# Sixteen transfers of v per pair instead of 28, four of them begun by ScalarE; scores in 32-query tiles; transposing writes turned into strided reads

## What is computed

```python
def hybrid_layer(x, g, w_in, rpb, w_dw, b_dw, ln_g, ln_b, w_pw, b_pw, w_out, pos):
    h = rms_norm(x, g)
    z = h @ w_in                                   # 1024 -> 3712 columns
    aq, ak, av, ag, bq, bk, bv, bg, ca, cb, cg = jnp.split(z, splits, axis=-1)
    ya = neighbourhood_attention(heads(aq, 4), heads(ak, 4), heads(av, 4), rpb) * silu(ag)
    yb = dilated_attention(rotary(heads(bq, 6), pos), rotary(heads(bk, 6), pos), heads(bv, 6)) * silu(bg)
    yc = conformer_conv(ca, cb, w_dw, b_dw, ln_g, ln_b, w_pw, b_pw) * silu(cg)
    return x + jnp.concatenate([ya, yb, yc], axis=-1) @ w_out
```

## Time and profile before

| | us |
|---|---|
| median of 3 runs | 555.41 |
| lowest, highest | 553.13, 556.37 |
| profiled execution, its own time | 554.33 |
| its span, first to last instruction | 552.7 |

### The profile page before, as it was taken

The page is one execution under the profiler, slowest core; times in us unless marked ns, Lnnn a source line. Parts: engine busy times, 40 slices in busy tenths (PEclk is TensorE's granted clock), DMA queues, the critical chain, the costliest instruction groups (busy, mean ns, idle before and its releaser), DMA issues.

```text
span 552.7 us, 9207 instructions
## 1 busy us (share of the span) xinstructions
PE 511.9 (93%) x3422; PEld 412.4 (75%) x3422; DVE 366.2 (66%) x733; ACT 244.9 (44%) x483; POOL 163.7 (30%) x224
## 2 busy tenths in 40 slices
PE   8999989399699999999999999948969999999995
PEld 7888767377587777778888877736748778787884
DVE  6889788389686486611639877773995866653333
ACT  6622355146255565523513215631643644763223
POOL 0113333112023555524411323221211335664201
PEclk9999999699899999999999999987999999999999
DMA  8626779637769698999503568882575979989973
GB/s 292 264 76 166 176 180 222 131 92 166 178 160 239 149 266 178 241 219 285 154 0 110 121 145 188 212 175 73 131 180 151 219 165 263 266 193 240 215 184 152
DMA packets 61931, 99.69 MB, mean 180 GB/s; under 512 B 25152, under 2 KB 38976, under 8 KB 61888
## 3 DMA queue, kind: packets, MB, share of 16 engines
q0 software_dynamic: 19648, 62.93, 50.7%
q1 hardware_dynamic: 41952, 36.00, 22.5%
q10 hardware_dynamic: 288, 0.19, 0.2%
HBM read 84.92 MB, written 4.72 MB: 162 GB/s over the span
## 4 chain that ended last, share of the span: by engine, by line
PE 76%; DMA 8%; issue 7%; DVE 5%; POOL 1%; SPq 1%; ACT 1%; POOLq 0%; DVEq 0%; ACTq 0%
PE acc L626 17%; PE acc L627 16%; PE acc L628 16%; DMA sq<-sq 4%; PE sc L742 3%; DMA w_lo<-w_out 3%; PE tp L765 3%; PE misc L796 2%; PE misc L791 2%; PE sc L688 1%; SPq L506 1%; PE sc L690 1%; PE sc L689 1%; PE sc L626 1%; PE sc L628 1%
## 5 line engine op out<-in xcount | busy, mean ns | idle before, releaser
L626 PE MATMUL acc<-act_hi,w_hi 128*128 128x512 f32 x480 | 194.3, 405 | 0.9 <-DMA w_lo<-w_out 0.9
L627 PE MATMUL acc<-act_hi,w_lo 128*128 128x512 f32 x480 | 187.6, 391 | 0.0
L628 PE MATMUL acc<-act_lo,w_hi 128*128 128x512 f32 x480 | 187.1, 390 | 0.0
L626 PEld LDWEIGHTS acc<-act_hi,w_hi 128*128 128x128 f32 x480 | 90.2, 188 | 22.1 <-issue 3.5
L628 PEld LDWEIGHTS acc<-act_lo,w_hi 128*128 128x128 f32 x480 | 90.2, 188 | 19.7
L627 PEld LDWEIGHTS acc<-act_hi,w_lo 128*128 128x128 f32 x480 | 90.3, 188 | 17.0 <-issue 0.5
L891 ACT ACTIVATE w_lo<-w_hi 128x1024 fp32r<-128x1024 f32 (+1 forms) x62 | 62.0, 1000 | 66.1 <-DMA w_hi<-w_out 39.2
L1316 DVE SCALAR_TENSOR_TENSOR y<-ub,par,y 128x512 f32<-128x512 f32 x90 | 68.1, 757 | 0.0
L953 ACT ACTIVATE prob<-prob,nmx 128x384 f32<-128x384 f32 (+1 forms) x80 | 45.2, 566 | 43.4 <-DVE nmx L1338 43.4
L1094 POOL DMA_DIRECT2D w_lo<-w_in x40 | 36.2, 905 | 94.9 <-ACT w_lo L891 94.3
L1316 DVE SCALAR_TENSOR_TENSOR ub<-ub,par 128x512 f32<-128x512 f32 x84 | 62.7, 747 | 0.0
(11 more groups left out here) (149 smaller groups left out, 756.0 us busy)
## 6 DMA issues: line engine op xcount, KB each, us to landing
w_hi<-w_in POOLq DMA_DIRECT2D x40, 512.0 KB, 5.3
w_lo<-w_in POOLq DMA_DIRECT2D x40, 512.0 KB, 6.1
w_hi<-w_out POOLq DMA_DIRECT2D x16, 512.0 KB, 6.7
w_lo<-w_out POOLq DMA_DIRECT2D x16, 512.0 KB, 7.0
pT<-w_in SPq DMA_DIRECT2D x15, 512.0 KB, 4.0
sq<-sq SPq DMA_DIRECT2D x48, 64.0 KB, 2.6
gf<-nabias SPq DMA_DIRECT2D x20, 128.0 KB, 5.4
v_way<-vs SPq DMA_DIRECT2D x8, 256.0 KB, 6.0
```

What stands on the lines that cost most here:

```text
L626: nc.tensor.matmul(to[:, :], w_hi[:, slot, k, :], a_hi[:, k, :], start=i == 0, stop=False)
L627: nc.tensor.matmul(to[:, :], w_lo[:, slot, k, :], a_hi[:, k, :], start=False, stop=False)
L628: last = nc.tensor.matmul(to[:, :], w_hi[:, slot, k, :], a_lo[:, k, :], start=False, stop=i == K - 1)
```

## The change

It has five parts.

- **Layout of v in HBM and the store.** `v_way` now keeps, for each of 32 rows, the four blocks of 32 partitions side by side. The store is four transfers of 32 partitions in place of one of 128.
- **Near loads.** SyncE's queue issues 12 transfers of a dilated pair, as before in shape, and no far ones.
- **Far loads.** `load_far` puts four transfers (32 partitions by 16 pieces of 32 elements each) in ScalarE's queue, at n = 6, 14 and 18 behind `norm`, in place of 16 on SyncE's. They go to a buffer of their own, `v_far`, and `values` waits for `far_moved` as well.
- **Scores.** Every product of scores is made for 32 queries at a time; near and far of one block follow each other.
- **Strided reads.** Seven access patterns on VectorE (v and the neighbourhood keys when emptied, rotated q and k) are walked in the order of the destination, so that they write neighbours and read with a step.

```diff
-        v = sb("v", [P, 2, 4, (NA_BLOCKS + CLASSES) * BLK])
+        v = sb("v", [P, 2, 4, NA_BLOCKS * BLK])
+        v_far = sb("v_far", [P, 2, 4, CLASSES * BLK])
-        v_way = nc.dram_tensor("v_way", (DEPTH, PAIRS, P, SEQ), F32, kind="Internal").ap()
+        v_way = nc.dram_tensor("v_way", (DEPTH, PAIRS, BLK, P // BLK, SEQ), F32, kind="Internal").ap()
...
         def by_class(t):
-            return t.rearrange("p (r a) -> p a r", r=CLASSES)
+            return t.rearrange("p (r a) -> p r a", r=CLASSES)
         def in_order(t):
-            return t.rearrange("p (a r) -> p a r", r=CLASSES)
+            return t.rearrange("p (a r) -> p r a", r=CLASSES)
...
             def store_v(l, g):
                 sp.wait_ge(v_blocks, PAIRS * l + g + 1)
-                sp.dma_start(v_way[l, g], v_buf(g)).then_inc(v_stored, 16)
+                for i in range(QUADS):
+                    sp.dma_start(v_way[l, g, :, i, :], v_buf(g)[BLK * i:BLK * (i + 1), :]).then_inc(v_stored, 16)
...
-                        t = v_way[l, g].rearrange("(i p) (r j c) -> j i p r c", p=BLK, r=CLASSES, j=QUADS)[j]
-                        for i in range(QUADS):
-                            sp.dma_start(to[:, i, FAR].rearrange("p (r c) -> p r c", r=CLASSES), t[i])\
-                                .then_inc(v_moved[g % 2], 16)
...
+                def product(b, r, h, first, end, keys_of):
+                    own, rows = slice(HD * h, HD * (h + 1)), slice(BLK * r, BLK * (r + 1))
+                    return nc.tensor.matmul(sc[2 * (b % 2) + h][rows, first:end],
+                                            queries[own, g % 2, b * P + BLK * r:b * P + BLK * (r + 1)],
+                                            keys_of(keys[own, g % 2, :]), start=True, stop=True)
...
+                        for r in range(CLASSES):
+                            for h in range(2):
+                                product(b, r, h, 0, NEAR, near)
+                        for r in range(CLASSES):
+                            for h in range(2):
+                                last = product(b, r, h, NEAR, DKEY, lambda t: t[:, P * r:P * (r + 1)])
                                 if r == CLASSES - 1:
+                                    last.then_inc(s_ready, 1)
...
                 if g < DPAIRS:
+                    pe.wait_ge(far_moved[g % 2], 16 * QUADS * (DPAIRS - 1 - g % 2) * l + 16 * QUADS * (g // 2 + 1))
...
+            def load_far(l, g):
+                act.wait_ge(v_stored, V_STORED * (PAIRS * l + g + 1))
+                if g >= 2:
+                    act.wait_ge(pv_done, PAIRS * l + g - 1)
+                elif l:
+                    act.wait_ge(pv_done, PAIRS * (l - 1) + DPAIRS)
+                for j in range(QUADS):
+                    t = v_way[l, g].rearrange("p i (r j c) -> j p (i r) c", r=CLASSES, j=QUADS)[j]
+                    act.dma_start(v_far[BLK * j:BLK * (j + 1), g % 2].rearrange("p i (r c) -> p (i r) c", r=CLASSES), t)\
+                        .then_inc(far_moved[g % 2], 16)
...
                     if 0 < n <= UNITS:
                         norm(l, n - 1)
+                    if n - 1 in V_LOADS and V_LOADS[n - 1] < DPAIRS:
+                        load_far(l, V_LOADS[n - 1])
```

More of the change, by code:

```diff
@@ L269, in build @@
         v_moved = [sem(f"v_moved{i}") for i in range(2)]
+        far_moved = [sem(f"far_moved{i}") for i in range(2)]
         x_blocks = sem("x_blocks")
@@ L390, in build @@
         NEAR_EVEN, NEAR_ODD = slice(0, QT * BLK), slice(QT * BLK, NA_BLOCKS * BLK)
-        FAR = slice(NA_BLOCKS * BLK, (NA_BLOCKS + CLASSES) * BLK)
+        V_STORED = 16 * QUADS
         def v_moves(g):
-            return (3 + QUADS) * QUADS if g < DPAIRS else QUADS
+            return 3 * QUADS if g < DPAIRS else QUADS
         def v_landed(l, g):
@@ L509, in store_v @@
                 sp.wait_ge(v_blocks, PAIRS * l + g + 1)
-                sp.dma_start(v_way[l, g], v_buf(g)).then_inc(v_stored, 16)
+                for i in range(QUADS):
+                    sp.dma_start(v_way[l, g, :, i, :], v_buf(g)[BLK * i:BLK * (i + 1), :]).then_inc(v_stored, 16)
             def load_v(l, g):
-                sp.wait_ge(v_stored, 16 * (PAIRS * l + g + 1))
+                sp.wait_ge(v_stored, V_STORED * (PAIRS * l + g + 1))
                 if PAIRS * l + g >= 2:
@@ L520, in load_v @@
                         low = NEAR_ODD.stop - NEAR_ODD.start
[L521 removed]
+                        t = v_way[l, g].rearrange("p i (j c) -> j p i c", j=QUADS)
                         sp.dma_start(to[:, :, NEAR_EVEN], t[j]).then_inc(v_moved[g % 2], 16)
@@ L731, in scores, with near @@
                     pe.wait_ge(m_ready, UNITS * l + n)
+                def product(b, r, h, first, end, keys_of):
[3 more added lines that the diff above has]
+                                            keys_of(keys[own, g % 2, :]), start=True, stop=True)
                 for b in range(b, b + 2):
[L734 to L737, removed]
+                    if g < DPAIRS:
+                        def near(t):
@@ L738, in scores @@
                             t = t.rearrange("p (r a) -> p r a", r=CLASSES)[:, :, NEAR_LO[b]:NEAR_LO[b] + 2 * PCLS]
[L739 to L747, removed]
+                            return t.rearrange("p r (u a) -> p u r a", u=2)
                         for r in range(CLASSES):
                             for h in range(2):
[L750 to L753, removed]
+                                product(b, r, h, 0, NEAR, near)
@@ L754, in scores @@
+                        for r in range(CLASSES):
+                            for h in range(2):
+                                last = product(b, r, h, NEAR, DKEY, lambda t: t[:, P * r:P * (r + 1)])
                                 if r == CLASSES - 1:
+                                    last.then_inc(s_ready, 1)
+                    else:
+                        for r in range(QUADS):
+                            for h in range(2):
+                                last = product(b, r, h, 0, NKEY,
+                                               lambda t: t[:, ROWS * NA_LO[b]:ROWS * NA_LO[b] + NKEY])
+                                if r == QUADS - 1:
@@ L790, in values @@
                         for i in range(QUADS):
-                            nc.tensor.matmul(of_class(ob[BLK * i:BLK * (i + 1), :], r), v_of(g, i, far_block(r)),
+                            nc.tensor.matmul(of_class(ob[BLK * i:BLK * (i + 1), :], r), v_far[:, g % 2, i, BLK * r:BLK * (r + 1)],
                                              of_class(pT[:, BLK * i // HD, 2, :], r), start=r == 0, stop=False)
@@ L1257, in empty_tile @@
                     if before is not None and before[0] >= 0:
-                        dve.wait_ge(v_stored, 16 * (PAIRS * before[0] + before[1] + 1))
+                        dve.wait_ge(v_stored, V_STORED * (PAIRS * before[0] + before[1] + 1))
                     nc.vector.transpose(v_blocked(g), vT.rearrange("p (m j t) -> p m j t", m=v_blocked(g).shape[1],
@@ L1347, in turn_p @@
                 if u == 0 and q == 2:
-                    dve.wait_ge(v_stored, 16 * PAIRS * (l + 1))
+                    dve.wait_ge(v_stored, V_STORED * PAIRS * (l + 1))
                 to = p_turned(q).rearrange("p (j u h t) -> p u h j t", j=QUADS, u=BATCH, t=BLK)[:, u]
```

12 lines of the change are left out of this document (5 added, 7 removed).

## The result

The changed kernel takes 530.3 us (median of 4, 525.61 to 532.15) beside 555.89 us of the kernel before on the same chip: ratio 0.952, 95% interval 0.943 to 0.961. The forecast was 524 us, range 515 to 539, and a faster kernel. The profiled execution took 528.64 us, its span is 526.8. One execution further down, 547.77 us of the kernel with all transfers on SyncE, was in a slower state of the chip and is left out of every number here.

A forecast was written before the change was run, and what follows sets the result against it. Bound: TensorE waiting for 28 transfers issued one behind the other. 554.3 - 28.9 (waits) - 6.9 (clock) + 1.5 (remaining wait) + 4.4 (ScalarE) - 1.7 (scores) = 522.7 us; as median 524 us, range 515 to 539.

The forecast's parts named there:

- The rival without effect: Before `values`: the wait is for the bank or the transposed probabilities, not v, so 555 us; chance 0.03.
- The clock: Matmuls of `values` behind the four waits: 17.98 us falls to 4 x 2.76 at full clock, -6.9 us.
- The near loads: SyncE's 12 near loads keep their shape: 1.6 us a group, 6.3 us for four, issued by 91.3 from 84.96.
- The remaining wait: Before the products of `values`: 1.5 us left for the whole program, bounds 0 and about 3 us per wait.
- What ScalarE pays: Store wait and four issues of 0.6 us delay the emptying of transposes: 2.2 us per layer, +4.4 us in all.
- I take 84.5: At n = 6: assumed time when the store of pair 0 has landed, making ScalarE 0.5 us late for the transposes.
- The slower rival: ScalarE's queue: issues of X us lose 12 X - 7 a layer; X = 2.3 gives 559 us; chance 0.03.
- The scores: Dilated pairs' score calls: one group of one form saves 0.14 us in each of 12 calls, -1.7 us.
- The strided reads: VectorE's strided SBUF reads: possibly 11 us of work saved, but TensorE never waits for it, so counted 0.
- The rival built on it: VectorE: each strided SBUF operand costs 0.4 us, an instruction 1.5 instead of 1.1; 530 us; chance 0.05.
- VectorE's cover: Without pair 1's wait VectorE is some 2 us behind but catches up by the scores: 0, bounds 0 and +6 us.
- One more sign: Sign of being right: SyncE's loads end some 12 us earlier relative to the first product of `values`.

The follow-up runs named there:

- the kernel with the later products: Changed kernel with far transfers one slot later and `values` of pairs 0 and 1 in the middle of the next half tile, gating behind taps: 522.10 us, ratio 0.940.

## Why the prediction was right, and where its terms were off

**What bounded the kernel** was named rightly. The wait before the products was the issuing of 28 transfers on one queue: with 16 on the same queue it is 17.0 us, with 12 there 2.1. The kernel with all 28 transfers on two queues, the last of them issued at 95.7 instead of 103.7 us, has no such wait, though TensorE also comes there later. The rival without effect is out.

**The clock** (-6.9 us) came as forecast where the waits went, 2.76 us at 1.00. What the step left out is that it works for any long wait: the new 4.18 us at the transposes cost 1.4 us behind them, and the kernel with 16 issues on ScalarE is some 12 us longer than its waits alone would make it.

**The near loads** were set at 0.58, 0.43 and 0.43 us; eleven of the twelve take 0.59 to 0.61 and one 0.67, so 7.7 us with the gaps instead of 6.3. It is the new layout in HBM, and not the second queue, that makes the small ones longer: their medians are 0.59 to 0.60 with all on SyncE as well, and 0.48 and 0.49 in the kernel with the old layout and two queues. The remaining wait was put at 1.5 us and is 2.1.

**What ScalarE pays** is the term that was mis-sized: +4.4 us forecast, +8.9 measured (10.5 less 1.6). The prediction names transposes that wait "for over 10 us in total" as a sign of being wrong; that sign came in the profiled execution, and was just missed (9.8) in the second one. An issue of 512 pieces was rightly taken at 0.6 us (median 0.649), and the number of pieces hardly counts. The wrong step was "I take 84.5" for the landing of the store of pair 0: it landed at 87.05. So TensorE waits 4.18 us behind n = 6 of the first layer where 0.5 was forecast. In that place the late landing is 2.5 of the 3.7 us between; 0.3 are the issues (2.88 instead of 2.6), and 0.8 come from TensorE, which got there at 87.38 instead of 88.15. This execution had the longest landing: 9.8 us from the first issue of the store to the first load, where the nine other profiled executions with a four-part store have 7.5 to 8.6. The forecast had 7.1. At the other places the waits are 1.25 (forecast 1.7) and 0.64 (0), and 1.09, 1.44 and 0.67 in the second layer, where 2.2 for all three was forecast. The 0.64 and 0.67 at n = 18 are the same term: the four-part store of pair 2 landed at 138.2 and held ScalarE there too. The 1.25 at n = 14 came without the wait for the store that the forecast had in it (landing at 127): the store had landed before ScalarE was free, and the issues and what stands behind them make it up.

**The slower rival** was priced by the right sum. Its 12 X - 7 us for a layer, with 16 issues of 0.65 us in place of four of X = 2.6, gives 24 x 2.6 - 14 = 48 us; the kernel made so waits 44.6 us in these places and is 3% slower than before. It didn't come to pass in the changed kernel because an issue of 512 pieces costs 0.65 us and not 2.2, and there are four of them.

**The scores** (-1.7 us) are right: 1.51 us a call where 1.52 was forecast, -2.0 us alone.

**The strided reads** (0) are right in the time. The mechanism had been left open, but "L1222 near 0.7 us" was named as a sign of being right, and it did not come: a read from SBUF with a step of 16 bytes costs nearly as much as the scattered write that it replaces. L1237 takes 1069 ns, L1222 took 1098:

```profile
L1237 DVE SCALAR_TENSOR_TENSOR vs<-acc,rstd 128x512 f32<-128x512 f32 x6 | 6.4, 1069 | 0.0
```

The rule of the Trainium skill ("SBUF — State Buffer", Door 1), that each access to a new line of 16 bytes pays a penalty, agrees for reads: 1.07 us against 0.69 when only PSUM is strided. The rival built on it put 0.4 us on each of two operands, 1.5 us in all; two of them take 1.07 us, as one does. It didn't price the change, since what it replaced paid about the same. VectorE's cover held: no wait of TensorE in the changed kernel names VectorE.

**The sum** against the profiled execution: forecast 522.7, measured 528.6. Of the 5.9 us between them, 4.5 are ScalarE's term, 0.6 the rest before the products, 1.1 a wait before the products of pair 4 that wasn't there before. The clock behind the wait would add 1.4 and the scores of the neighbourhood pairs take off 0.3, so these terms make 7.3 us and overshoot by 1.4, which stays unexplained. One more sign was weaker than said: SyncE's loads end 7.5 us before the product, where they ended 2.6 us before it, so 4.9 us earlier and not 12. The median lies 1.7 us above that execution.

**What stays open.** The landing of v and ScalarE's blocked queue stand so close that moving work off one gives most of it to the other: the five kernels that shift the far transfers or the products have sums of 9.7 to 10.8 us. With these left where the change puts them the sums are 12.6, 12.4, 11.4 and 10.6 us, so the difference is hardly larger than that between single executions. Why the kernel with the later products has a median 4 us under its profiled execution isn't settled; a profile of a faster execution of it was not taken. And a store that lands sooner, from which both queues would gain, wasn't found: the one way tried landed later.

## What to carry to other kernels

When an engine waits for many small transfers, look first at how long one queue takes to issue them: 28 took 18.7 us to issue here and each landed within 7.1. Merging them and giving a part to a second queue both help, but the second queue belongs to an engine with its own work, and there two things cost: the wait in front of the transfers (4.6 us at n = 6) and their number (16 held the queue for 11.2 us, four for 2.9), but hardly their size. Put them where what they wait for has surely come, and count what stands behind them. After such a wait is gone, price the next one with the clock: behind 4.2, 8.7 and 9.5 us of idle TensorE some 1.4, 1.9 and 2.9 us more were lost.

## What the hardware showed unexpectedly

- From the new layout an issue takes 0.59 to 0.61 us for 64 or 128 pieces on SyncE's queue and 0.65 us for 512 on ScalarE's (medians). From the old layout the same 64 pieces take 0.43 to 0.46 us. Four in a row stretched to 4.7 us in one run, while the DMA engines moved some 270 GB/s.
- VectorE reads PSUM with a step of 16 bytes at full speed (688 ns for 512 columns), and SBUF with a step of 16 or 256 bytes in 1.07 us, no better than a scattered write (1.10).
- One store of 128 partitions whose outer dimension in HBM is 4 took 8.7 to 10.6 us, the last of four stores of 32 partitions 5.2 to 8.2.
- Products of 256 columns in eight tiles of 64 by 32 run side by side as well as in two of 64 by 128: 1.02 against 1.06 us for a call of a neighbourhood pair. With near and far products in one form a dilated call takes 1.51 us, in two forms 1.66.
